# Block 0's experts chosen in two halves during the queries; scores of blocks 1 to 3 kept in SBUF for a later top-k

## Chip, cores, metric

One NeuronCore of a Trainium2 chip runs one launch. The metric is the device time of that launch in microseconds. Before the change three runs gave 1512.22, 1512.45 and 1513.83 us (median 1512.45).

## What is computed

A decoder layer for 512 tokens of width 1024, all in float32: RMS norm, one input projection, an mLSTM group and a latent-attention group, an output projection and a residual. The change touches only what follows, the PEER layer:

```python
qry = (xb @ w_q).reshape(TB, 8, 256)                 # 8 heads
s1 = einsum('thd,nd->thn', qry[..., :128], keys_1)   # 128 keys each
s2 = einsum('thd,nd->thn', qry[..., 128:], keys_2)
v1, i1 = top_k(s1, 16); v2, i2 = top_k(s2, 16)
cand = v1[..., :, None] + v2[..., None, :]           # 256 pairs
sc, ci = top_k(cand, 16)
idx = i1[ci // 16] * 128 + i2[ci % 16]               # 16384 experts
gate = softmax(sc)
act = gelu(einsum('thed,td->the', u_table[idx], xb))
y = einsum('the,thed->td', gate * act, v_table[idx])
```

## The kernel before, in words

The program is written out by hand for five engines, each with its own order, and kept in step by semaphores. The 512 tokens are four blocks of 128 (t = 0 to 3).

**Front** (0 to 290 us): projections, both attention groups, the output projection, and the normed h2 of each block. PSUM banks are handed round in the order of the list JOBS, eight at a time: a job's bank is free when the engine that takes it has read the job eight places earlier.

**Queries** (290 to 396 us). For each of 8 heads h: ScalarE rounds a part of w_q to float32r (wq_hi, round_q), GpSimd makes the rest (wq_lo, L709), TensorE makes two query tiles in three passes of 8 matmuls each (L1745, 24 matmuls a tile; the wait on wqlo_ready stands ahead of the first pass), and then the scores of all four blocks with 8 small matmuls (L1933). The scores stay in two PSUM banks ("s12", h, i), and VectorE takes from them, for each block and head, the 16 best of 128 keys twice (MAX8, FIND_INDEX8, MATCH_REPLACE8; L1440 to L1450). I call this one top-k.

**choose(t)** (L1456 to L1520, VectorE) makes out of the best keys of a block the 16 best experts of each head: sums (cand), a second top-k, and a search for the experts' numbers in which picked, 128x3200, is written and reduced twice, for 4 heads each time. choose(0) follows the last top-k and ends with idx0, for which GpSimd waits. choose(1) to choose(3) are cut into pieces that VectorE puts between other work, at PIECE_SIZE ns for each expert block.

**Dense products, pre** (blocks n = 0 to 71, 396 to about 670 us): tokens of blocks 1 to 3 (all but 32 tokens of block 1) are multiplied with all 16384 rows of u, 128 rows a block. For block n SyncE loads u_raw, ScalarE rounds it (u_hi, L981), GpSimd or VectorE makes u_lo (L718, L1526), TensorE runs 24 matmuls (L1952), the last 8 of which need u_lo, and ScalarE applies Gelu (L1019), for which TensorE waits two blocks later. GpSimd makes u_lo of the blocks below POOL_FIRST = 16, from SHARE_FROM = 20 on the even ones.

**Gathers and dots**: for block 0 (128 slots, "a") and for the 32 tokens left of block 1 ("b") the chosen rows of u are fetched: GpSimd issues an indirect DMA of 128 rows of 4 KB (gather_u, L734) into one of 8 buffers u_rows, VectorE multiplies and sums them with h2 (dot, L1543). A gather waits until the dot that used its buffer is done. The list DOTS says after which block which dots stand. The "a" dots read h2 of block 0 from two PSUM banks (h2_first, copied there by ScalarE, L1008), the "b" dots from SBUF (h2x).

**Main** (blocks 72 to 119, to 952 us) adds one-hot matmuls that spread the gates (L1598, L1991), **post** (blocks 120 to 127, to 986 us) prepares the second product, which fills TensorE to 1508 us: v_hi (L1095), v_lo (L1620), w (L1636, L1637), w_lo. DOTS puts two "a" dots after each of the blocks 120 to 123.

Of the kernel before, what the change touches and what calls it, by code (L numbers as in the profile page):

```python
# [92 lines left out]
POOL_FIRST, SHARE_FROM = 16, 20  # L93
# [9 lines left out]
DOTS = [""] * POST + ["aa"] * 4 + [""] * 4  # L103
# [7 lines left out]
assert "".join(DOTS).count("b") == NE  # L111
assert "".join(DOTS).count("a") == SLOTS
ORDER = [(kind, "".join(DOTS)[:x].count(kind)) for x, kind in enumerate("".join(DOTS))]
DOTS_PRE = len("".join(DOTS[:PRE]))
# [16 lines left out]
def front_jobs():  # L131
# [44 lines left out]
ENGINE_OF = dict(JOBS)  # L176

# [9 lines left out]
def build(nc, a):  # L187
    ctx = ExitStack()
    with ctx:
# [80 lines left out]
        wq_raw = [at(f"wq_raw{i}", kb, [P, KD, UNIT]) for i, kb in enumerate((42, 117.5, 106))]  # L270
        wq_hi = [at(f"wq_hi{i}", kb, [P, KD, UNIT], F32R) for i, kb in enumerate((126, 66))]
        wq_lo = [at(f"wq_lo{i}", kb, [P, KD, UNIT], F32R) for i, kb in enumerate((194, 74))]
        qryT = at("qryT", 186, [P, 3, S])
# [15 lines left out]
        pay_f = at("pay_f", 94, [P, 2, PH, TOPK])  # L289
# [195 lines left out]
        def _(sp):  # L485
# [31 lines left out]
            for h in range(PH):  # L517
                if h == 1:

                    sp.wait_ge(mixed_ready, 1)  # L520
# [3 lines left out]
                if h >= 3:  # L524

                    sp.wait_ge(wqlo_ready, h - 2)
# [14 lines left out]
            for j in range(1, 4):  # L541
                load_u(j, j)
# [126 lines left out]
        def _(pool):  # L669
# [36 lines left out]
            for h in range(PH):  # L706

                pool.wait_ge(wqhi_ready, h + 1)
                nc.gpsimd.tensor_tensor(wq_lo[h % 2][:], wq_raw[h % 3][:], wq_hi[h % 2][:].bitcast(F32),  # L709
                                        ALU.subtract).then_inc(wqlo_ready, 1)  # L710

            def split_u(n):

                pool.wait_ge(uhi_ready, n + 1)
                if n == 3:

                    arrived(pool, ("qry", PH - 1, 1))
# [3 lines left out]
            def gather_u(s):  # L721
# [3 lines left out]
                kind, x = ORDER[s]  # L725
                if kind == "b" and x == 0:
# [11 lines left out]
            for n in range(POOL_FIRST):  # L738
                split_u(n)
# [1358 lines left out]
```

## Time and profile before

| | |
|---|---|
| median of 3 runs | 1512.45 us |
| span of the profiled execution | 1512.2 us |
| runs beside it | 1512.22, 1512.45, 1513.83 us |
| TensorE busy | 97% (1473.2 us) |
| VectorE / ScalarE / GpSimd busy | 77% / 42% / 44% |
| mean granted clock of TensorE | 0.992 |
| chain that ended last | PE 73%, DVE 10%, DMA 9%, POOL 5% |

The profiled execution has no time of its own in the record beside its span; the fastest of the runs is 1512.22 us. In the profile PE is TensorE, DVE VectorE, ACT ScalarE, POOL GpSimd, SP SyncE. A timeline's row has start, duration, engine, line, operation, out<-in and shape; a bracket gives the idle time before it and what ended it.

### The profile page before, as it was taken

The page shows a single profiled execution, that of the slowest core. Times are in us where ns is not written, and L with a number is a line of the kernel's source. Part 1 is how long each engine was busy: PE and PEld are TensorE (multiplying, and loading weights), DVE is VectorE, ACT ScalarE, POOL GpSimd, SP SyncE. Part 2 cuts the span into 40 slices and gives each one's busy share as a digit, 9 for nine tenths or more (in the row PEclk, how much of TensorE's full clock was granted, in tenths as well). Part 3 has the DMA queues.
Part 4 walks back from the last instruction along what each step waited for, and adds up shares of the span by engine and source line. Part 5 has one row for each costly group of instructions (what it writes and reads, how often), then busy time and mean ns, then how long its engine had stood idle before and what let it go on. Part 6 is the DMA issues. An engine that isn't in the chain of part 4 may idle for free.

```text
span 1512.2 us, 23375 instructions
## 1 busy us (share of the span) xinstructions
PE 1473.2 (97%) x8069; PEld 1313.0 (87%) x8069; DVE 1161.3 (77%) x2378; ACT 640.6 (42%) x1058; POOL 665.2 (44%) x387
## 2 busy tenths in 40 slices
PE   6999989899999999999999999999999999999999
PEld 6879648788999999999999999988888888888887
DVE  4528473368999999879898889768878877877876
ACT  5363453222333333447777767434333224223221
POOL 3223150233586677865545545234443443443341
PEclk9999989999999999999999999999999999999999
DMA  6400202220569989999999999799999999999993
GB/s 205 147 29 1 112 1 70 88 74 25 173 207 354 328 313 341 415 356 360 354 361 362 349 365 397 293 333 382 383 354 352 347 352 347 354 347 349 351 345 123
DMA packets 182810, 408.19 MB, mean 270 GB/s; under 512 B 12725, under 2 KB 108725, under 8 KB 181209
## 3 DMA queue, kind: packets, MB, share of 16 engines
q1 hardware_dynamic: 141144, 256.36, 48.0%
q0 software_dynamic: 41600, 151.03, 26.3%
q8 instruction: 32, 0.52, 0.1%
q14 instruction: 34, 0.27, 0.0%
HBM read 359.03 MB, written 48.30 MB: 269 GB/s over the span
## 4 chain that ended last, share of the span: by engine, by line
PE 73%; DVE 10%; DMA 9%; POOL 5%; issue 2%; ACT 1%; SPq 0%; DVEq 0%; ACTq 0%; POOLq 0%
PE banks L1952 16%; PE banks L1745 16%; PE banks L2020 12%; PE banks L2021 12%; PE banks L2022 12%; DMA u_rows<-in_u,idx 7%; DVE gate_rows L1598 3%; POOL u_lo L718 3%; DVE u_rows L1543 2%; POOL u_rows L734 2%; DVE oh L1594 1%; DVE u_lo L1526 1%; PE banks L1933 1%; DMA u_raw<-in_uT 1%; PE banks L1796 1%
## 5 line engine op out<-in xcount | busy, mean ns | idle before, releaser
L766 POOL DMA_INDIRECT v_rows<-in_v,idx x128 | 203.5, 1590 | 324.4 <-DVE x_res L1682 274.6
L2020 PE MATMUL banks<-v_hi,w_hi 128*128 128x512 f32 x768 | 298.9, 389 | 0.0
L2021 PE MATMUL banks<-v_lo,w_hi 128*128 128x512 f32 x768 | 298.8, 389 | 0.0
L2022 PE MATMUL banks<-v_hi,w_lo 128*128 128x512 f32 x768 | 298.8, 389 | 0.0
L1095 ACT ACTIVATE v_hi<-v_raw 128x1024 fp32r<-128x1024 f32 x128 | 126.4, 1050 | 326.6 <-PE banks L2022 292.3
L734 POOL DMA_INDIRECT u_rows<-in_u,idx x160 | 190.4, 1190 | 139.7 <-DVE z L1543 106.3
L1620 DVE TENSOR_TENSOR v_lo<-v_raw,v_hi 128x1024 fp32r<-128x1024 f32 x128 | 153.5, 1221 | 95.2 <-ACT v_hi L1095 95.2
L718 POOL TENSOR_TENSOR u_lo<-u_raw,u_hi 128x1024 fp32r<-128x1024 f32 x66 | 163.9, 2486 | 90.4 <-ACT u_hi L981 49.7
L1952 PE MATMUL banks<-h_lo,u_hi 128*128 128x352 f32 x1024 | 197.5, 327 | 0.0
L1952 PE MATMUL banks<-h_hi,u_hi 128*128 128x352 f32 x1024 | 190.6, 328 | 0.0
L1952 PE MATMUL banks<-h_hi,u_lo 128*128 128x352 f32 x1024 | 187.0, 324 | 3.3 <-DVE u_lo L1526 3.3
L1543 DVE CUSTOM_DVE_ANT_0 u_rows<-u_rows,banks 128x1024 f32<-128x1024 f32 x128 | 152.2, 1220 | 28.7 <-DMA u_rows<-in_u,idx 28.7
L1952 PEld LDWEIGHTS banks<-h_hi,u_lo 128*128 128x128 f32 x1024 | 169.2, 188 | 3.6 <-DVE u_lo L1526 3.6
L2022 PEld LDWEIGHTS banks<-v_hi,w_lo 128*128 128x128 f32 x768 | 144.1, 188 | 30.2
L2020 PEld LDWEIGHTS banks<-v_hi,w_hi 128*128 128x128 f32 x768 | 144.1, 188 | 30.1 <-DVE v_lo L1620 0.3
L2021 PEld LDWEIGHTS banks<-v_lo,w_hi 128*128 128x128 f32 x768 | 144.1, 188 | 29.8
L1952 PEld LDWEIGHTS banks<-h_lo,u_hi 128*128 128x128 f32 x1024 | 167.0, 188 | 0.0
L1952 PEld LDWEIGHTS banks<-h_hi,u_hi 128*128 128x128 f32 x1024 | 166.6, 189 | 0.0
L1682 DVE SCALAR_TENSOR_TENSOR x_res<-v_rows,w,x_res 128x1024 f32<-128x1024 f32 x128 | 163.8, 1280 | 0.9
L981 ACT ACTIVATE u_hi<-u_raw 128x1024 fp32r<-128x1024 f32 x122 | 128.1, 1051 | 20.8 <-DMA u_raw<-in_uT 17.1
L1019 ACT ACTIVATE act_out<-banks 128x352 f32<-128x352 f32 x116 | 53.0, 457 | 143.8 <-PE banks L1952 133.8
L1991 PE MATMUL banks<-gate_rows,oh 128*128 128x128 f32 x768 | 101.3, 275 | 2.7 <-DVE gate_rows L1598 2.7
(269 smaller groups left out, 2072.6 us busy)
## 6 DMA issues: line engine op xcount, KB each, us to landing
u_raw<-in_uT SPq DMA_DIRECT2D x128, 512.0 KB
v_raw<-in_v SPq DMA_DIRECT2D x128, 512.0 KB
gate_scratch<-stage SPq DMA_DIRECT2D x12, 2048.0 KB
gates<-gate_scratch SPq DMA_DIRECT2D x29, 768.0 KB
act_scratch<-act_out SPq DMA_DIRECT2D x116, 176.0 KB
act_in<-act_scratch SPq DMA_DIRECT2D x29, 704.0 KB, 6.7
wi_raw<-in_w_in SPq DMA_DIRECT2D x8, 1024.0 KB, 8.8
wq_raw<-in_w_q SPq DMA_DIRECT2D x8, 1024.0 KB, 5.5
```

The source lines that it names most:

```text
L718: nc.gpsimd.tensor_tensor(u_lo[:, n % 4, :, :], u_raw[:, n % 4, :, :], u_hi[:, n % 4, :, :].bitcast(F32), ALU.subtract).then_inc(ulo_pool, 1)
L734: nc.gpsimd.indirect_dma_start(u_rows[U_SLOT[s]][:], None, a["u"], bass.IndirectOffsetOnAxis(ap=at_x, axis=0)).then_inc(ug_in[U_SLOT[s]], 16)
L766: nc.gpsimd.indirect_dma_start(v_rows[s % V_ROWS][:], None, v_flat, bass.IndirectOffsetOnAxis(ap=idx0[:, s:s + 1], axis=0)).then_inc(vg_in ...
L981: nc.scalar.activation(u_hi[:, j % 4, :, :], u_raw[:, j % 4, :, :], ACT.Copy).then_inc(uhi_ready, 1)
L1543: nc.vector.tensor_tensor_reduce(rows[:], rows[:], h2, 1.0, 0.0, ALU.mult, ALU.add, z[:, x:x + 1]).then_inc(dot_done, 1)
L1620: nc.vector.tensor_tensor(v_lo[q][j][:], v_raw[:, j, :], v_hi[q][:, j, :].bitcast(F32), ALU.subtract).then_inc(vlo_ready, 1)
L1682: nc.vector.scalar_tensor_tensor(out=x_res[:, 0, :], in0=v_rows[n % V_ROWS][:], scalar=w0[:, n:n + 1], in1=x_res[:, 0, :], op0=ALU.mult, o ...
L1745: last = mm(o, lhs(x, k), rhs(y, k), start=n == k == 0, stop=n == 2 and k == KD - 1)
L1952: last = mm(o, u[:, q, k, :], h2[:, k, T1:], start=m == 0, stop=m == PER_BLOCK - 1)
L2020: mm(y, w, v_hi[q][:, j, ds], start=first and j == 0, stop=False)
L2021: mm(y, w, v_lo[q][j][:, ds], start=False, stop=False)
L2022: end = mm(y, w_lo[q][:, j, t * P:(t + 1) * P], v_hi[q][:, j, ds], start=False, stop=last and j == GROUP - 1)
```

## The change

Scores of block 0 get a bank of their own ("s0", h), which VectorE reads as before and frees halfway through its top-k; those of block 1 ("s13", h, 0) and of blocks 2 and 3 ("s13", h, 1) are copied by ScalarE to scores_1 and scores_23 in SBUF. In the queries VectorE does the top-k of block 0 and of block 1 only. After head 3 it runs choose on heads 0 to 3 of block 0; then, after each of the heads 4 to 7, six dots, 24 in all, which read h2 of block 0 from SBUF (h2_nat). The other half of choose(0), the last top-k of block 1, the top-k of blocks 2 and 3 and choose(1) to choose(3) become pieces of the pre stage; FREE_SIZE = 85000 ns of them come before block 30. GpSimd makes u_lo of all blocks below 32. 24 "a" dots leave their later places: 16 of the pre stage and the 8 of post; 3 "b" dots move from pre to main. wq_lo is written over wq_raw, buffers move, and h2x is loaded only when 24 dots are done.

```diff
-POOL_FIRST, SHARE_FROM = 16, 20
+POOL_FIRST, SHARE_FROM = 32, 32
+EARLY = 24
+EARLY_STEP = 6
...
-DOTS = [""] * POST + ["aa"] * 4 + [""] * 4
+DOTS = [""] * E_BLOCKS
...
-for _n in [*range(PRE - 25, PRE, 2), *range(PRE + 1, PRE + 32, 2), PRE + 4, PRE + 14, PRE + 24]:
+for _n in [*range(PRE - 19, PRE, 2), *range(PRE + 1, PRE + 32, 2), *range(PRE + 4, PRE + 28, 4)]:
     DOTS[_n] += "b"
-for _n in [*range(PRE - 14, PRE, 4), *range(PRE + 32, POST)]:
+for _n in range(PRE + 32, POST):
     DOTS[_n] += "a"
+FREE_SIZE = 85000
...
-        jobs += [(("s12", h, i), "D") for i in range(2)]
+        jobs += [(("s0", h), "D")] + [(("s13", h, i), "A") for i in range(2)]
...
@@ SyncE
-            sp.wait_ge(wqlo_ready, PH)
+            arrived(sp, ("qry", PH - 2, 1))
             load_u(0, 0)
-            arrived(sp, ("qry", PH - 2, 1))
...
                     sp.wait_ge(h2x_saved, 16)
+                    sp.wait_ge(dot_done, EARLY)
...
@@ GpSimd
-            for n in range(POOL_FIRST):
-                split_u(n)
-            pool.wait_ge(idx_ready, 1)
-            s = 0
+            for h in range(PH - 1):
+                split_query(h)
+            pool.wait_ge(idx_ready, 1)
+            for s in range(U_ROWS):
+                gather_u(s)
+            split_query(PH - 1)
+            for s in range(U_ROWS, U_ROWS + 2 * EARLY_STEP):
+                gather_u(s)
+            split_u(0)
+            split_u(1)
+            for s in range(U_ROWS + 2 * EARLY_STEP, U_ROWS + 3 * EARLY_STEP):
+                gather_u(s)
+            split_u(2)
+            for s in range(U_ROWS + 3 * EARLY_STEP, U_ROWS + EARLY):
+                gather_u(s)
+            for n in range(3, POOL_FIRST):
+                split_u(n)
...
@@ VectorE
+                if n < EARLY:
+                    h2 = h2_nat[:, 0, :]
...
-            for _ in choose(0):
-                pass
+            for h in range(PH // 2):
+                top_k(0, h)
+                if h:
+                    top_k(1, h - 1)
+            for _ in choose(0, 0, PH // 2):
+                pass
+            top_k(1, PH // 2 - 1)
+            for h in range(PH // 2, PH):
+                top_k(0, h)
+                if h > PH // 2:
+                    top_k(1, h - 1)
+                for _ in range(EARLY_STEP):
+                    dot()
```

**GpSimd, from the split of the last query to the splits of the products.** Before: all query splits, 16 product splits (u_lo), then the wait for idx and the gathers (idx is idx0, in_u the table u).

```order
L709 TENSOR_TENSOR wq_lo_112<-wq_raw_107,wq_hi_110 128x2048 [waits wqhi_ready]
L718 TENSOR_TENSOR u_lo<-u_raw,u_hi 128x1024 [waits uhi_ready] x3
L718 TENSOR_TENSOR u_lo<-u_raw,u_hi 128x1024 [waits bank_done,uhi_ready]
L718 TENSOR_TENSOR u_lo<-u_raw,u_hi 128x1024 [waits uhi_ready] x12
L734 DMA u_rows_150<-in_u,idx_146 128x1024 [waits idx_ready]
L734 DMA u_rows_151<-in_u,idx_146 128x1024
```

After the change, the same place ("..." stands for the gathers of the buffers between):

```order
L729 TENSOR_TENSOR wq_lo_109<-wq_raw_106,wq_hi_113 128x2048 [waits wqhi_ready]
L754 DMA u_rows_154<-in_u,idx_150 128x1024 [waits idx_ready]
...
L754 DMA u_rows_161<-in_u,idx_150 128x1024
L729 TENSOR_TENSOR wq_lo_110<-wq_raw_107,wq_hi_114 128x2048 [waits wqhi_ready]
L754 DMA u_rows_154<-in_u,idx_150 128x1024 [waits dot_done]
...
L754 DMA u_rows_157<-in_u,idx_150 128x1024 [waits dot_done]
L735 TENSOR_TENSOR u_lo<-u_raw,u_hi 128x1024 [waits uhi_ready] x2
...
L754 DMA u_rows_155<-in_u,idx_150 128x1024 [waits dot_done]
L735 TENSOR_TENSOR u_lo<-u_raw,u_hi 128x1024 [waits uhi_ready]
...
L754 DMA u_rows_161<-in_u,idx_150 128x1024 [waits dot_done]
L735 TENSOR_TENSOR u_lo<-u_raw,u_hi 128x1024 [waits uhi_ready] x29
```

The first 32 gathers now stand ahead of the product splits: 8 ahead of the split of query 7, 12 more ahead of u_lo of blocks 0 and 1, 6 ahead of block 2, 6 ahead of block 3 (the first of the 29). From the ninth on each gather waits for a dot.

**VectorE, from the numbers of the experts on.** Before, choose(0) ends with the cast to idx after all 32 head and block pairs have had their top-k, and choose(1) and a product split follow:

```order
L1494 TENSOR_TENSOR picked<-pay,sc_f 128x3200 [waits dve_step]
L1498 TENSOR_REDUCE e_f<-picked 128x64 [waits dve_step]
L1503 CAST idx_146<-e_f 128x128 [waits dve_step]
L1456 TENSOR_SCALAR pay_f<-best_i 128x128
L1457 CAST pay_f<-best_i 128x128
```

After the change, the end of the first half of choose(0), the start of a top-k of block 1 from SBUF, of one of block 0 from PSUM, and the six dots (ISA with h_nat; h_nat is the name at the address of h2_nat):

```order
L1548 TENSOR_TENSOR picked<-pay,sc_f 128x3200
L1552 TENSOR_REDUCE e_f<-picked 128x64 [waits dve_step]
L1557 CAST idx_150<-e_f 128x64 [waits dve_step]
L1491 MAX best_v<-scores_116 128x8 [waits bank_freed_scalar]
...
L1491 MAX best_v<-banks 128x8 [waits bank_done,dve_step]
...
L1599 ISA u_rows_154,z_151<-u_rows_154,h_nat 128x1024 [waits ug_in0,dve_step]
...
L1599 ISA u_rows_159,z_151<-u_rows_159,h_nat 128x1024 [waits ug_in5]
L1599 ISA z_151 128x1
L1491 MAX best_v<-banks 128x8 [waits bank_done]
```

After each six dots come two top-k, the first of which waits for TensorE's scores of the next head; the last six dots follow the top-k of head 7.

## Rows read from the trace of the kernel before

**Rows 1.** The chain of waits, query and pre stage: start, us, what, matmuls

```profile
309.79 1.78 PE banks L1933 x16
...
374.97 10.90 PE banks L1745 x48
...
395.85 205.22 PE banks L1952 x1296
```

**Rows 2.** Two stretches: busy us of PE, PEld, DVE, ACT, POOL; clock, DMA share, GB/s

```profile
340.00:360.00 20.00, 20.00 (x98) 16.87 (x97) 17.93 (x105) 5.40 (x5) 7.01 (x2) 1.00 0.07 26
640.00:660.00 20.00, 20.00 (x127) 19.98 (x127) 14.56 (x25) 7.17 (x10) 12.03 (x8) 1.00 0.96 380
```

**Rows 3.** VectorE's timeline: two top-k and choose(0)

```profile
310.72 0.50 DVE L1440 MAX8 best_v<-banks 128x8 f32<-128x128 f32 x2 [19.10 <-PE banks L1933]
...
313.62 0.50 DVE L1440 MAX8 best_v<-banks 128x8 f32<-128x128 f32 x2
...
410.48 0.78 DVE L1456 TENSOR_SCALAR pay_f<-best_i 128x128 f32<-128x128 uint32 x1
411.89 3.18 DVE L1465 TENSOR_TENSOR cand<-best_v 128x128 f32<-128x128 f32 x7
...
423.19 3.48 DVE L1494 TENSOR_TENSOR picked<-pay,sc_f 128x3200 f32<-128x3200 f32 x1
426.71 3.48 DVE L1498 TENSOR_REDUCE e_f<-picked 128x64 f32<-128x3200 f32 x1
...
497.88 0.99 DVE L1465 TENSOR_TENSOR cand<-best_v 128x128 f32<-128x128 f32 x7
```

**Rows 4.** GpSimd's timeline: a query split, and a gather (its issue)

```profile
357.58 4.57 POOL L709 TENSOR_TENSOR wq_lo<-wq_raw,wq_hi 128x2048 fp32r<-128x2048 f32 x1 [8.09 <-ACT wq_hi L782]
...
450.33 0.93 POOL L734 DMA_INDIRECT u_rows<-in_u,idx  x1 [0.30 <-issue]
```

**Rows 5.** Timelines of VectorE and GpSimd where h2x dots meet GpSimd

```profile
601.01 1.21 DVE L1543 CUSTOM_DVE_ANT_0 u_rows<-u_rows,h2x 128x1024 f32<-128x1024 f32 x1
...
600.16 1.74 POOL L734 DMA_INDIRECT u_rows<-in_u,idx  x1 [0.31 <-issue]
...
695.34 1.22 DVE L1543 CUSTOM_DVE_ANT_0 u_rows<-u_rows,banks 128x1024 f32<-128x1024 f32 x1
...
696.48 1.40 DVE L1543 CUSTOM_DVE_ANT_0 u_rows<-u_rows,h2x 128x1024 f32<-128x1024 f32 x1
...
694.39 2.42 POOL L718 TENSOR_TENSOR u_lo<-u_raw,u_hi 128x1024 fp32r<-128x1024 f32 x1 [1.35 <-DVE opened L1563]
```

**Rows 6.** A DMA's landing: tile h2x; and u_rows in the chain of waits

```profile
DMA to landing us min/median/max: 3.0/3.1/4.2
...
766.89 10.20 DMA u_rows<-in_u,idx
```

**Rows 7.** ScalarE's timeline: copy of h2, then the first Gelu

```profile
398.58 1.03 ACT L1008 ACTIVATE banks<-h_nat 128x1024 f32<-128x1024 f32 x1 [2.95 <-DVEq L1452]
...
401.90 0.47 ACT L1019 ACTIVATE act_out<-banks 128x352 f32<-128x352 f32 x1
```

**Rows 8.** TensorE's timeline after two long waits

```profile
290.39 3.78 PE L1745 MATMUL banks<-h_hi,wq_hi 128*128 128x512 f32 x8 [0.69 <-ACT h_hi L938]
...
298.75 1.98 PE L1745 MATMUL banks<-h_hi,wq_hi 128*128 128x512 f32 x8
...
975.28 2.50 PE L1952 MATMUL banks<-h_hi,u_lo 128*128 128x352 f32 x8 [3.28 <-DVE u_lo L1526]
...
979.50 1.43 PE L1952 MATMUL banks<-h_lo,u_hi 128*128 128x352 f32 x8
```

**Rows 9.** Timelines of ScalarE and VectorE ahead of TensorE's wait at 972 us

```profile
967.01 2.00 ACT L1095 ACTIVATE v_hi<-v_raw 128x1024 fp32r<-128x1024 f32 x2
...
970.06 2.35 DVE L1620 TENSOR_TENSOR v_lo<-v_raw,v_hi 128x1024 fp32r<-128x1024 f32 x2
...
974.00 1.22 DVE L1526 TENSOR_TENSOR u_lo<-u_raw,u_hi 128x1024 fp32r<-128x1024 f32 x1
```

More of the change, by code:

```diff
@@ L517, in _ @@
             for h in range(PH):
-                if h == 1:
+                if h == 0:
                     sp.wait_ge(mixed_ready, 1)
@@ L725, in gather_u @@
                 kind, x = ORDER[s]
+                if kind == "a" and x == SLOTS // 2:
+                    pool.wait_ge(idx_ready, 2)
                 if kind == "b" and x == 0:
@@ L1454, in choose, with top_k @@
-            def choose(t):
-                step(nc.vector.tensor_scalar(pay_f[:, 0, :, :], best_i[:, 0, t, :, :], float(NK), None, ALU.mult))
-                step(nc.vector.tensor_copy(pay_f[:, 1, :, :], best_i[:, 1, t, :, :]))
+            def top_k(t, h):
+                j = ("s13", h, 0 if t == 1 else 1) if t else ("s0", h)
+                if t:
+                    emptied(dve, j)
+                else:
+                    arrived(dve, j)
+                from_at = scores[t][:, h, :] if t else bank(j)
+                sc = [from_at[:, s * NK:(s + 1) * NK] for s in range(2)]
+                bv = [best_v[:, s, t, h, :] for s in range(2)]
+                bi = [best_i[:, s, t, h, :] for s in range(2)]
+                for s in range(2):
+                    step(nc.vector.max(bv[s][:, 0:8], sc[s]))
+                settle()
+                for s in range(2):
+                    step(nc.vector.max_index(bi[s][:, 0:8], bv[s][:, 0:8], sc[s]))
+                    step(nc.vector.match_replace(best_tmp[:, s, :], bv[s][:, 0:8], sc[s], LOWEST))
+                settle()
+                if not t:
+                    dve.sem_inc(freed["D"], 1)
+                for s in range(2):
+                    step(nc.vector.max(bv[s][:, 8:16], best_tmp[:, s, :]))
+                settle()
+                for s in range(2):
+                    step(nc.vector.max_index(bi[s][:, 8:16], bv[s][:, 8:16], best_tmp[:, s, :]))
+                settle()
@@ L1567, in splits_and_dots, with routing @@
                     dot()
[L1569 to L1574 removed]
+            def routing():
+                pieces = choose(0, PH // 2, PH)
+                for size in HALF_SIZES:
+                    next(pieces)
+                    yield size
+                assert next(pieces, 0) == 0
+                top_k(1, PH - 1)
+                yield TOPK_SIZE
+                for t in range(1, TB):
+                    if t > 1:
+                        for h in range(PH):
+                            top_k(t, h)
+                            yield TOPK_SIZE
+                    pieces = choose(t)
+                    for size in CHOOSE_SIZES:
+                        next(pieces)
+                        yield size
+                    assert next(pieces, 0) == 0
+            work, done = routing(), 0
+            for n in range(POOL_FIRST - 2, PRE):
+                while done < FREE_SIZE + (n - POOL_FIRST + 3) * PIECE_SIZE:
+                    size = next(work, None)
+                    if size is None:
+                        break
+                    done += size
                 splits_and_dots(n)
```

170 lines of the change are left out of this document (86 added, 84 removed).

## Prediction

> **What bounds the kernel now.** I read the page first: TensorE is busy for 97% of the span, VectorE for 77%, the others for less than half, and TensorE's amount of work (matmuls, columns, order) is not touched by the change. So the change can gain only where TensorE waits, and loses whatever new wait it gives TensorE. Second the chain of waits: from 309.79 us on, a head of the query stage is two tiles (10.90 us) and its scores (1.78 us), 12.68 us, one after the other without a gap, and from 395.85 us the first 54 blocks (1296 matmuls) take 205.22 us, 3.80 us a block [rows 1]. Third the windows: in the queries TensorE is busy 20.00 of 20 us while VectorE has 17.93, and at 640 us VectorE is down to 14.56 [rows 2]. VectorE's top-k, the work that the change moves, thus lies beside TensorE's work already, and moving it gains nothing by itself. The one wait ahead of the second product is in post: 3.28 us for u_lo of block 125, and after it TensorE runs slowly for 4 us [rows 8]. What can go wrong lies in the queries: the change puts work on two queues, GpSimd's and VectorE's, on whose results TensorE waits at once.
>
> **Step 1: when the first half of choose(0) ends.** Scores of block 0, head 3, are there at 309.79 + 3 x 12.68 + 0.55 (their quarter of 1.78 us and 0.1) = 348.4 [rows 1]. Two top-k of 2.90 us each [rows 3] bring VectorE to 354.2. The small steps of choose(0) took 423.19 - 410.48 = 12.7 us for 8 heads, of them 2.2 because cand took 3.18 us there and 0.99 at 497.88, and some 0.5 at pay_f; half of the 10.0 left and a little for fixed cost is 5.4. picked and its reduction are 3.48 us each and stay whole for 4 heads [rows 3]. Without a collision that is 354.2 + 5.4 + 7.0 + 0.2 = 366.8. But picked reads two tiles in SBUF and comes at 359.6, inside GpSimd's split of query 6 (357.58 to 362.15 [rows 4]); I let it wait (see step 3): 369.3.
>
> **Step 2: GpSimd.** From 369.4 it issues 8 gathers at 0.93 + 0.30 us [rows 4], the last few against dots, to 381.6, and only then the split of query 7, 4.57 us [rows 4]: 386.2. TensorE has that tile due at 374.97 + 5.45 = 380.4 [rows 1]: the first new wait, 5.9 us (1.0 without collisions).
>
> **Step 3: the loop of gathers and dots.** Gather s waits for dot s-8, and 32 gathers stand ahead of the split of block 3; so this split waits for dot 23, the last early one. Between 369.3 and dot 23 VectorE has eight top-k, 8 x 2.90 = 23.2 us, and 24 dots at 1.14 us (695.34 to 696.48 [rows 5]), 27.4 us: 419.9 with no wait at all. Now the collisions. An "a" dot read h2 from PSUM; the early ones read both operands from SBUF, like the dots with h2x. The gather that met one took 1.74 us in place of 0.93 and ended 0.89 us after that dot's start, and a dot with h2x that met a product split took 1.40 in place of 1.21 [rows 5]. So I walk the two queues forward with three rules: a dot, picked and a GpSimd split exclude each other; a gather's end waits for the first 0.87 us of a dot; data land 3.3 us after the issue, a little over the 3.1 us of h2x [rows 6]. The walk: dots 0 to 5 end at 381.9, 6 to 11 at 395.8, 12 to 17 (behind the splits of blocks 0 and 1) at 412.8, 18 to 23 at 426.0; u_lo of blocks 0, 1, 2, 3 is ready at 406.0, 409.3, 419.2 and **431.2**. TensorE needed the last at 395.85 + 3 x 3.80 + 2.53 (16 of 24 matmuls) = 409.8. The delay is 431.3 - 409.8 = **21.5 us**. On TensorE it shows as 5.9 (query 7), 1.9 (block 0), 7.0 (block 2) and 6.8 (block 3). The 7.0 is ScalarE's: its copy of h2 needs the bank of head 7's scores of block 0, which VectorE frees at 414.4, and from copy to first Gelu pass 3.8 us [rows 7].
>
> **Bounds of step 3.** Without any collision the same walk gives 12.0 us (dot 23 at 417.3, u_lo of block 3 at 421.6). With each dot holding off a gather for its whole 1.14 us it gives 27.5. With landings of 8 us (in main they reach 10.20 [rows 6]) it gives 25.9. I take 21.5, because the two rows that show collisions are of the same instruction pair as here. The floor is firm: head 7's scores come at 399.1, then stand two top-k, six dots, a gather and a split, 5.8 + 6.8 + 1.2 + 2.4 us, which with 0.1 makes 415.4 and a delay of 5.6 us even if nothing else ever waited.
>
> The Trainium skill (SBUF — State Buffer, section "SBUF: two separate sides") says that VectorE and GpSimd share a port pair as an exclusive lock: an instruction of VectorE with two SBUF inputs and a GpSimd one block each other, for the whole instruction of whichever starts first. By that rule the sum would carry 27.5 us in place of 21.5; the gather above went on 0.3 us before its dot ended, so the trace agrees with the lock and only in part with its length.
>
> **Step 4: the clock.** After waits of this kind TensorE ran slowly: the first query tile took 298.75 - 290.39 = 8.4 us in place of 5.4, and after 972 us 16 matmuls took 4.22 us (975.28 to 979.50) in place of 2.53 [rows 8]. After the last new wait I add the middle of 3.0 and 1.7, **2.4 us**; after the waits before it the slow stretch lies inside the next wait and costs nothing.
>
> **Step 5: post.** The dots of blocks 120 to 123 go. The last two stand ahead of v_lo at 970.06 and so of u_lo at 974.00, for which TensorE waited. ScalarE has the rounded v for it at 968.0 [rows 9], so v_lo can start at 968.1 and 1.9 of the 3.28 us go: **-1.9**. What is left, 1.4 us, is far shorter than the waits behind which a slow stretch is on record, so I count step 4's 1.7 us as gone too: **-1.7**. At worst the gate rows from HBM, which VectorE needs next, come late and both stay: 0.
>
> **At nothing.** The top-k of blocks 2 and 3 (16 x 2.90 = 46 us), the other half of choose(0) and one top-k more come to VectorE in pre; 10 product splits, 16 "a" and 3 "b" dots and the first half leave it. From 426 us on it has until block 72 half of choose(0) 12.6, 17 top-k 49.3, three choose of some 26, 21 splits 25.6, 52 dots 59.3 and the norms 5: 230 us, and block 72 starts near 693: 37 us spare. The cover before was the idle share at 640 us [rows 2]; if it fails, u_lo of odd blocks comes late, a few us. GpSimd's 16 more splits of 2.4 us fit under 3.8 us a block. ScalarE's 16 score copies go beside queries. SyncE's new wait for the 24 dots (426) has the load of block 8 behind it, which waits for u_lo of block 4 (434) anyway and is due on TensorE at 448: no cost. Three "b" dots more in main: within VectorE's gaps.
>
> **Sum** against the profiled span: 1512.2 + 21.5 + 2.4 - 1.9 - 1.7 = **1532.5 us**; the span lies 0.25 us below the median of the runs.
>
> **Rivals.** (a) As above, 1532.5: 0.46. (b) The collisions cost next to nothing, so that 12.0 stands for 21.5: 1523.0. For it: the pairs of rows that show them are few, and other instructions may have stretched them; against it: the two pairs of rows in [rows 5]. 0.22. (c) The lock at full length: 27.5 us, 1538.5; for it, picked and splits stretch each other too; 0.22. (d) The early part reaches TensorE only at the floor, 5.6 us, no slow stretch: 1512.2 + 5.6 - 3.6 = 1514.2; it needs VectorE never late, against the sum of 419.9: 0.04. (e) Faster: gathers and dots keep ahead of TensorE, and only post changes: 1508.6. The point at which this decides is u_lo of block 3 at 409.8 us; dot 23 would have to end by 406.0, 13.9 us sooner than VectorE's own work allows: 0.04. (f) The change doesn't do what it says, its gathers landing so late that the dots wait for data (8 us): 25.9 us, 1536.9: 0.02.
>
> **Numbers.** A difference under 0.2% (3.0 us) can't be told from no change here. Faster is (e), 0.04; within is (d), 0.04; slower the rest, 0.92. The range leaves out (d) and (e), and goes from 1519, which is (b) without the clock's 2.4 us and 1.6 us off its choose, to 1541, (c) with the upper end of the clock (0.6) and half of step 5 (1.8).
>
> **What would show it.** In the profile after: the split of query 7 ends at 386 and TensorE waits for it at 380; a wait for Gelu or for the h2 copy ahead of block 2; u_lo of block 3 ready near 431 and TensorE's wait there named POOL u_lo; a granted clock of 0.5 behind it; gathers of 1.3 to 1.8 us among the early dots; the wait at 972 (then near 995) of 1.4 us. The forecast is wrong if the first 54 blocks start within 3 us of 395.85 and go at 3.80 each.

## The result, and the profile after

The changed kernel takes 1538.38 us (median of 4 runs, 1537.48 to 1540.2) against 1512.34 us before (4 runs, 1510.18 to 1513.83): ratio 1.0179, 95% interval 1.016 to 1.0199. It is slower by 1.8%. The profiled execution after has a span of 1536.6 us, 24.4 more than before, at a mean granted clock of 0.984.

TensorE's waits, from the view of the waits (total, times, longest us):

```profile
...
PE banks L2040 <- ACT act_out L1067: 9.5, 1, 9.5
PE banks L2040 <- POOL u_lo L735: 7.2, 2, 6.2
...
PE banks L1834 <- POOL wq_lo L729: 5.2, 1, 5.2
...
PE banks L2040 <- DVE u_lo L1580: 1.0, 1, 1.0
```

Four new ones stand in the first three rows shown, 21.9 us together. The last row is what is left of the wait for u_lo of block 125 [rows 8]. TensorE's timeline shows where they lie: the first tile of query 7, the third pass of block 0, the first of block 2, the third of block 3, and post.

```profile
384.54 3.78 PE L1834 MATMUL banks<-h_hi,wq_hi 128*128 128x512 f32 x8 [5.16 <-POOL wq_lo L729]
...
392.84 1.95 PE L2021 MATMUL banks<-keysT,qryT 128*128 128x128 f32 x16
...
406.56 1.54 PE L2040 MATMUL banks<-h_hi,u_lo 128*128 128x352 f32 x8 [1.04 <-POOL u_lo L735]
...
421.42 2.68 PE L2040 MATMUL banks<-h_hi,u_hi 128*128 128x352 f32 x8 [9.52 <-ACT act_out L1067]
...
435.84 2.72 PE L2040 MATMUL banks<-h_hi,u_lo 128*128 128x352 f32 x8 [6.17 <-POOL u_lo L735]
...
443.67 1.43 PE L2040 MATMUL banks<-h_hi,u_hi 128*128 128x352 f32 x8
...
1001.44 1.54 PE L2040 MATMUL banks<-h_hi,u_lo 128*128 128x352 f32 x8 [1.05 <-DVE u_lo L1580]
```

Before, the third pass of block 3 started at 409.62 us (TensorE's timeline: 395.60 is the start of block 0). So 26.2 us are lost by then, although the first scores came 1.05 us sooner (308.58 against 309.63). From 435.84 to 443.67 four passes took 7.83 us; at 1.267 each (3.80 us a block, [rows 1]) they would take 5.07, so the slow clock behind the last wait cost 2.8 us. The windows show it and its two forerunners; the columns are as in [rows 2], the third number from the right is the granted clock:

```profile
384.00:388.00 4.00, 3.46 (x8) 2.78 (x9) 4.00 (x7) 0.00 (x0) 3.54 (x3) 0.50 0.66 227
...
420.00:424.00 4.00, 2.58 (x9) 2.61 (x10) 3.90 (x14) 3.51 (x5) 2.48 (x2) 0.50 0.94 341
436.00:440.00 4.00, 4.00 (x14) 4.00 (x15) 4.00 (x1) 0.46 (x1) 4.00 (x2) 0.50 0.94 268
```

0.50 is the lower of the two clocks, 1.2 GHz, and each time TensorE had just stood still. In post the wait is 2.2 us shorter than in [rows 8], and no slow stretch follows (the pass takes 1.54 us where it took 2.50), which gives 1.7 us. 26.2 + 2.8 - 2.2 - 1.7 = 25.1 us, against 24.4 measured. The 0.7 us between them can be placed. From block 6 to block 110 the change is 28.98 us behind at each block's start, so nothing in pre or in most of main adds to the delay. Then two waits for gate rows, 2.7 us before, are gone, but TensorE's passes behind them are slower in the change (1.33 us in place of 1.27, see the last section), which takes back some 2 us. Ahead of the wait in post the change is 28.3 us behind (998.90 against 970.57), and 28.3 - 2.2 - 1.7 = 24.4.

The two queues behind this, GpSimd's and VectorE's timelines. GpSimd's rows are three gathers, the split of query 7 and two gathers among dots. VectorE's first row is a small copy in choose(0), the others are the fourth of the early dots, which met that split, then the fifth, the sixth and the seventh:

```profile
368.93 1.12 POOL L754 DMA_INDIRECT u_rows<-in_u,idx  x1 [7.83 <-DVE idx L1557]
...
372.85 0.94 POOL L754 DMA_INDIRECT u_rows<-in_u,idx  x1 [0.30 <-issue]
...
378.02 1.94 POOL L754 DMA_INDIRECT u_rows<-in_u,idx  x1 [0.30 <-issue]
379.99 4.50 POOL L729 TENSOR_TENSOR wq_lo<-wq_raw,wq_hi 128x2048 fp32r<-128x2048 f32 x1
384.65 1.75 POOL L754 DMA_INDIRECT u_rows<-in_u,idx  x1 [0.16 <-issue]
386.71 1.98 POOL L754 DMA_INDIRECT u_rows<-in_u,idx  x1 [0.30 <-issue]
```

```profile
358.97 2.17 DVE L1540 COPY tops<-sc_v 128x4 f32<-128x4 f32 x1
...
379.33 6.25 DVE L1599 CUSTOM_DVE_ANT_0 u_rows<-u_rows,h_nat 128x1024 f32<-128x1024 f32 x1 [0.18 <-DMA u_rows<-in_u,idx]
...
385.51 1.21 DVE L1599 CUSTOM_DVE_ANT_0 u_rows<-u_rows,h_nat 128x1024 f32<-128x1024 f32 x1
...
386.66 1.22 DVE L1599 CUSTOM_DVE_ANT_0 u_rows<-u_rows,h_nat 128x1024 f32<-128x1024 f32 x1
...
393.68 1.22 DVE L1599 CUSTOM_DVE_ANT_0 u_rows<-u_rows,h_nat 128x1024 f32<-128x1024 f32 x1
```

The dot at 379.33 ends at 385.58, 1.1 us after the split, though its row begins 0.66 us before the split's: the start of a row does not tell which of two goes first. The gather at 386.71 began 0.05 us after a dot and ended at 388.69, 0.8 us after that dot's end. From 379.3 to the end of dot 23 at 428.5 VectorE has no wait of note.

### The profile page after: what moved, and what is told of

Same layout as the page of the kernel before. It is cut to its first block, busy times and chain, and to the rows that moved or that the text cites. A ratio compares the mean times of both kernels' runs of the same rounds, so it can differ in the third digit from the quotient of the medians.

```text
span 1536.6 us, 23312 instructions
## 1 busy us (share of the span) xinstructions
PE 1481.7 (96%) x8069; PEld 1320.3 (86%) x8069; DVE 1176.1 (77%) x2383; ACT 648.4 (42%) x1074; POOL 691.3 (45%) x397
## 4 chain that ended last, share of the span: by engine, by line
PE 89%; DVE 7%; ACT 1%; POOL 1%; issue 1%; DMA 1%; DVEq 0%; ACTq 0%
PE banks L2040 31%; PE banks L1834 13%; PE banks L2109 11%; PE banks L2107 11%; PE banks L2108 11%; PE banks L2078 6%; DVE u_rows L1599 2%; POOL u_rows L754 1%; PE banks L1885 1%; DVE wo_lo L1402 1%; PE banks L1944 1%; PE banks L1963 0%; PE banks L1969 0%; PE banks L1891 0%; DMA u_rows<-in_u,idx 0%
## 5 line engine op out<-in xcount | busy, mean ns | idle before, releaser
L735 POOL TENSOR_TENSOR u_lo<-u_raw,u_hi 128x1024 fp32r<-128x1024 f32 x76 | 191.4, 2524 | 91.4 <-DVE opened L1631 64.3
L1014 ACT ACTIVATE u_hi<-u_raw 128x1024 fp32r<-128x1024 f32 x122 | 128.1, 1051 | 15.5 <-DMA u_raw<-in_uT 14.6
L1599 DVE CUSTOM_DVE_ANT_0 u_rows<-u_rows,banks 128x1024 f32<-128x1024 f32 x104 | 122.8, 1214 | 4.8 <-DMA u_rows<-in_u,idx 4.6
L1687 DVE TENSOR_SCALAR gate_rows<-consts,tab 128x128 f32<-128x128 f32 x384 | 105.2, 356 | 11.1 <-PE banks L2078 6.9
```

What stands on the lines that cost most here:

```text
L735: nc.gpsimd.tensor_tensor(u_lo[:, n % 4, :, :], u_raw[:, n % 4, :, :], u_hi[:, n % 4, :, :].bitcast(F32), ALU.subtract).then_inc(ulo_pool, 1)
L1014: nc.scalar.activation(u_hi[:, j % 4, :, :], u_raw[:, j % 4, :, :], ACT.Copy).then_inc(uhi_ready, 1)
L1599: nc.vector.tensor_tensor_reduce(rows[:], rows[:], h2, 1.0, 0.0, ALU.mult, ALU.add, z[:, x:x + 1]).then_inc(dot_done, 1)
```

## The experiments

They ran on three chips, on which even the kernel before spread over 1506 to 1518 us, and the changed kernel, on one of them, over 1534 to 1549. So the totals are read with their intervals, and the early part is read from each trace: the start of block 3's third pass, 409.62 us before and 435.84 in the change.

**The change again.** Unchanged.

> The changed kernel as it is, beside the others on this chip. The runs here spread over 10 us in place of 3, and in some profiles a u block took 4.00 us in place of 3.80 at an unchanged granted clock. If that is of the chip and the moment, the change lies at 1535 to 1545 us here with block 3's third pass at 435 to 439 us; if block 3's third pass lies elsewhere, the trace of the change that the other runs are read against was not typical.

Measured: 1544.76 us (1534.48 to 1549.06), ratio 1.023 (1.0198 to 1.0262).

```profile
406.12 1.54 PE L2040 MATMUL banks<-h_hi,u_lo 128*128 128x352 f32 x8 [2.13 <-POOL u_lo L735]
...
421.00 2.69 PE L2040 MATMUL banks<-h_hi,u_hi 128*128 128x352 f32 x8 [9.54 <-ACT act_out L1067]
...
435.41 2.72 PE L2040 MATMUL banks<-h_hi,u_lo 128*128 128x352 f32 x8 [5.88 <-POOL u_lo L735]
```

The same waits to within 1.1 us, and block 3 at 435.4. The early part repeats; the total is what varies here.

**Query 7 first.** Is the wait for wq_lo a loss of its own?

```diff
-            for h in range(PH - 1):
+            for h in range(PH):
                 split_query(h)
             pool.wait_ge(idx_ready, 1)
             for s in range(U_ROWS):
                 gather_u(s)
-            split_query(PH - 1)
```

> The changed kernel, but GpSimd splits the weights of query 7 ahead of the first eight gathers. Theory A, the chain of dots decides: VectorE had no idle time between the first gathers and dot 23, so the end of dot 23 and with it u_lo of block 3 hardly move; TensorE's 5.2 us for wq_lo go, and the waits behind them (Gelu 9.5, u_lo 6.2) grow by about as much. What can be won is the slow clock behind the wait for wq_lo and the 5.0 us by which that split stretched a dot, less the 4.6 us by which the gathers now start later: 1534 to 1539 us. Rival B, TensorE's waits simply add up, each with its own cause: the 5.2 us go and so do some 2.7 us of slow clock behind them: 1530.5 us. If A holds, the wait for wq_lo is gone from the trace and the wait for Gelu is 12 to 15 us.

Measured: 1548.37 us (1541.48 to 1556.53), ratio 1.0225 (1.0163 to 1.0286).

```profile
392.45 3.75 PE L1833 MATMUL banks<-h_hi,wq_hi 128*128 128x512 f32 x8 [5.49 <-issue]
...
425.12 2.68 PE L2039 MATMUL banks<-h_hi,u_hi 128*128 128x352 f32 x8 [7.39 <-ACT act_out L1066]
...
439.37 2.71 PE L2039 MATMUL banks<-h_hi,u_lo 128*128 128x352 f32 x8 [6.13 <-POOL u_lo L735]
```

The wait for wq_lo is gone, and TensorE waits 5.5 us at the second tile of query 7 instead. The profile names no releaser. In the code that tile needs the bank of head 5's scores of block 0, which VectorE frees in a top-k behind the first six dots. Block 3 comes 3.5 us later, as the first gather is issued at 374.3 in place of 368.9. Theory A holds in substance (nothing is won), though not for the wait for Gelu, which was to grow and fell to 7.4 us; B is out. The total lies above A's 1539 as well: in the profiled execution TensorE was 32.8 us behind the kernel before at block 5 and 44.6 at block 64, as each block took 4.00 us in place of 3.80 (last section).

**Top-k before dots.** The same question for the wait for Gelu.

```diff
                 top_k(0, h)
+                if h == PH - 1:
+                    for _ in range(EARLY_STEP):
+                        dot()
                 if h > PH // 2:
                     top_k(1, h - 1)
-                for _ in range(EARLY_STEP):
-                    dot()
+                if h != PH - 2:
+                    for _ in range(EARLY_STEP):
+                        dot()
```

> The changed kernel, but VectorE does the six dots behind head 6 only after the top-k of block 0, head 7, so that the bank of these scores is free sooner for ScalarE's copy of h2. Theory A, the waits of TensorE are stations of one chain: the wait for Gelu falls from 9.5 to 3 us or less, and the waits for u_lo of blocks 2 and 3 grow by 4 to 9 us; block 3's third pass starts within 3 us of the 435.8 us that it had. Rival B, the wait for Gelu is a cause of its own: block 3's third pass starts at 428 us or sooner.

Measured: 1538.63 us (2 runs), ratio 1.0179 (1.0148 to 1.0211).

```profile
406.05 2.48 PE L2044 MATMUL banks<-h_hi,u_lo 128*128 128x352 f32 x8 [3.48 <-POOL u_lo L735]
...
422.56 2.71 PE L2044 MATMUL banks<-h_hi,u_lo 128*128 128x352 f32 x8 [6.79 <-POOL u_lo L735]
...
434.38 2.72 PE L2044 MATMUL banks<-h_hi,u_lo 128*128 128x352 f32 x8 [5.79 <-POOL u_lo L735]
```

The 9.5 us for Gelu are gone, the waits for u_lo have grown from 7.2 to 16.0 us in all, and block 3 moved by 1.5 us. The waits are stations of one chain.

**Dots with one input.** What do the collisions cost? These 24 dots leave out the multiplication with h2.

```diff
+                if n < EARLY:
+                    nc.vector.tensor_reduce(z[:, x:x + 1], rows[:], AX_X, ALU.add).then_inc(dot_done, 1)
+                    return
```

> The changed kernel, but the 24 early dots only sum the gathered row, with one input in SBUF; the multiplication with h2 is left out of these 24. Number, place and order of gathers, dots and splits stay. Theory A, collisions of two-input instructions with GpSimd make up about half of the delay (two dots were stretched by 5.0 and 2.2 us, and nine gathers of 24 took 1.7 to 2.0 us in place of 0.94): dots are near 1.1 us each, the gathers 0.94, u_lo of block 3 comes some 9 to 13 us sooner, and the whole takes 1523 to 1529 us. Rival B, the order of the two queues does it and collisions are part of the picture only: 1535 us or more. Rival C, a reduction with one input holds GpSimd off as well: gathers of 1.7 us and more remain, and the time is within 2 us of 1538.

Measured: 1535.09 us (1528.22 to 1540.41), ratio 1.0145 (1.0094 to 1.0195). From the groups of instructions between 368 and 434 us (busy us, mean ns), first the change, then this kernel:

```profile
L754 POOL DMA_INDIRECT u_rows<-in_u,idx x32 | 40.0, 1251 | 20.6 <-issue 8.4 <-DVE idx L1557 7.8 <-DVE z L1599 4.4
L1599 DVE CUSTOM_DVE_ANT_0 u_rows<-u_rows,h_nat 128x1024 f32<-128x1024 f32 x24 | 35.4, 1526 | 1.3 <-issue 1.0 <-DMA u_rows<-in_u,idx 0.2
```

```profile
L754 POOL DMA_INDIRECT u_rows<-in_u,idx x32 | 30.2, 944 | 17.8 <-issue 8.7 <-DVE idx L1557 7.8 <-DVE z L1600 1.1
L1600 DVE TENSOR_REDUCE z<-u_rows 128x1 f32<-128x1024 f32 x24 | 27.8, 1212 | 2.1 <-DMA u_rows<-in_u,idx 1.8 <-issue 0.2
```

The gathers take 0.94 us in the mean: GpSimd spends 9.8 us less on them and VectorE 7.6 less on its dots. That excludes C. But block 3 comes at 429.71, only 6.1 us sooner, and not 9 to 13 as in A. Part of the rest went into something new, in TensorE's timeline in the middle of the last query tile:

```profile
399.42 0.40 PE L1837 MATMUL banks<-h_hi,wq_lo 128*128 128x512 f32 x1 [2.32 <-issue]
400.14 0.40 PE L1837 MATMUL banks<-h_hi,wq_lo 128*128 128x512 f32 x1 [0.33 <-issue]
```

TensorE stops there for 3.0 us in all with no releaser, and the pass goes on slowly; another stop of this kind, 2.3 us, stands ahead of block 2. What they are stays open. In sum the collisions are worth about 6 us here, more if these stops are a chance event; 20 us of the delay stay without them, which is B's side: the order of the two queues does most of it. The total of 1535 us is above theory A's 1529 and at B's lower end; the single runs reach from 1528 to 1540.

**Half of the early dots.** Three behind each head in place of six.

```diff
-EARLY = 24
-EARLY_STEP = 6
+EARLY = 12
+EARLY_STEP = 3
...
+for _n in range(31, 67, 3):
+    DOTS[_n] += "a"
...
-FREE_SIZE = 85000
+FREE_SIZE = 100000
```

> The changed kernel with 12 early dots in place of 24, three behind each head in place of six; the other 12 go to pre, one every third block from 31 on, and VectorE's free time ahead of block 30 is counted as 100 us in place of 85. Theory A, the chain through both queues decides: GpSimd has 20 gathers ahead of the split of block 3 in place of 32 and VectorE 12 dots less (14 to 18 us), so that VectorE has idle time and u_lo of block 3 is ready near 414 to 419 us; the wait for wq_lo stays, as the first eight gathers still stand ahead of it. 1516 to 1524 us. Rival B, the loss is one of place (any gather in the queries) and not of number: 1530 us or more.

Measured: 1546.06 us (1544.05 to 1551.33), ratio 1.0224 (1.0198 to 1.025). Block 3's third pass starts 15.9 us sooner than in the change, and that of block 2 waits 1.8 us:

```profile
413.97 1.54 PE L2042 MATMUL banks<-h_hi,u_lo 128*128 128x352 f32 x8 [1.83 <-POOL u_lo L737]
...
419.99 1.55 PE L2042 MATMUL banks<-h_hi,u_lo 128*128 128x352 f32 x8 [0.35 <-POOL u_lo L737]
```

For the early part A is right: each of the 12 dots and gathers less is worth 1.3 us, where A had about 1. The total is far off, and TensorE's timeline tells where most of it went. TensorE is 10.5 us behind the kernel before up to block 32 and 27.7 us at block 36, as there is a wait in block 32:

```profile
545.49 2.71 PE L2042 MATMUL banks<-h_hi,u_lo 128*128 128x352 f32 x8 [15.03 <-POOL u_lo L737]
```

GpSimd had waited 23.9 us for "opened", the mark by which VectorE lets it make u_lo of block 32. I read that as my 100 us of routing ahead of block 30 and tried again with 95:

```diff
-FREE_SIZE = 100000
+FREE_SIZE = 95000
...
-PIECE_SIZE = 1800
+PIECE_SIZE = 1500
```

> The run with half of the early dots again (12 in the queries, three behind each head, 12 in pre), without what spoiled it: there VectorE did 100 us of routing ahead of block 30 and opened GpSimd's split of block 32 fifteen us late. Now 95 us, and 1.5 us of routing per block behind it in place of 1.8. Theory A, the early loss goes with the number of gathers ahead of the split of block 3, about 1 us for each: block 3's third pass near 424 us again, against 435.8 in the change and 409.6 before, no long wait at block 32, and 1522 to 1528 us. Rival B, pre has no room for 12 dots beside the moved top-k: block 3 as in theory A, and behind it waits for u_lo or gate rows that sum to 5 us or more, 1530 us and above.

Measured: 1539.7 us (1535.4 to 1546.02), ratio 1.0196 (1.0163 to 1.0229). Block 3's third pass starts at 420.68, after a wait of 4.11 us. The 424 us that the theories gave for it fit block 4's third pass of the run before (423.90); block 3's was at 419.99. At block 32 there are still 9.1 us:

```profile
541.88 2.71 PE L2042 MATMUL banks<-h_hi,u_lo 128*128 128x352 f32 x8 [9.13 <-POOL u_lo L737]
```

In the change itself, block 32 is close as well: GpSimd's timeline has

```profile
542.53 2.42 POOL L735 TENSOR_TENSOR u_lo<-u_raw,u_hi 128x1024 fp32r<-128x1024 f32 x1 [6.97 <-DVE opened L1631]
```

so u_lo of block 32 is ready at 544.95, and TensorE takes it at 548.80 (435.84 + 29 x 3.80 and the 2.8 us of slow clock). Only 3.9 us are spare, and that while TensorE is 29 us late. With half of the early dots most of the gain is lost again at block 32: TensorE is 12.8 us behind ahead of it and 25.4 at block 36, and then 31.0 at block 64, as its blocks take 4.00 us (last section). So theory B holds for the total, by that wait. That a smaller FREE_SIZE would mend it was not tried.

**No early dots, twice.** First all 24 behind the queries.

```diff
-                for _ in range(EARLY_STEP):
-                    dot()
...
+            for n in range(POOL_FIRST):
+                split_u(n)
+                if 4 <= n < 4 + EARLY:
+                    gather_u(U_ROWS + n - 4)
...
+            for _ in range(EARLY):
+                at = done
+                while done < at + TOPK_SIZE:
+                    done += next(work)
+                dot()
```

> The changed kernel with its 24 early dots behind the query stage: all query and the first four u splits on GpSimd come ahead of the further gathers, then one gather per block, and VectorE does one such dot per top-k in pre, reading h2 from PSUM. The scores in SBUF, the choice of block 0 in halves and the empty post stay. Theory A, the early gathers and dots are the whole loss: the waits for wq_lo, Gelu and u_lo of blocks 0 to 3 are gone, post's gain stays (2.2 and 1.8 us by the trace of the change) and the front's 1.0 us: 1507 to 1510 us. Rival B, the scores through ScalarE and the top-k in pre cost something of their own: then 1513 us or more, with TensorE waiting for u_lo of an odd block between 32 and 72, or for tri.

Measured: 1536.63 us (1531.51 to 1542.44), ratio 1.0146 (1.0106 to 1.0186). Block 3's third pass starts at 409.72, as before. So the early gathers and dots are the whole of the early loss. But then TensorE waits nine times for u_lo, 17.1 us in all, and GpSimd's timeline says why:

```profile
436.70 0.95 POOL L753 DMA_INDIRECT u_rows<-in_u,idx  x1 [4.19 <-DVE z L1588]
437.68 2.35 POOL L734 TENSOR_TENSOR u_lo<-u_raw,u_hi 128x1024 fp32r<-128x1024 f32 x1
```

A gather waits for the dot that frees its buffer, and the next split stands behind it. The second version has a gather behind every second split only, and 12 of the dots in later blocks (not in GpSimd's way until block 31).

```diff
+                if n >= 6 and n % 2 == 0 and n < 6 + 2 * EARLY:
+                    gather_u(U_ROWS + n // 2 - 3)
...
+                while done < at + 2 * TOPK_SIZE:
```

> The changed kernel with no dot in the queries: the weights of query 7 first, then eight gathers, and 12 further gathers of block 0, one behind every second u split from block 6 on; VectorE does those 12 dots after every second top-k in pre, 12 more stand in pre, one every third block from 31 on. It mends what the run with all 24 behind the queries did: there GpSimd had a gather behind each split and TensorE waited nine times for u_lo, 17.1 us. Theory A, GpSimd's load was all that was wrong there: no wait for u_lo of more than 1 us up to block 31, and the post stage as in the change: 1507 to 1512 us. Rival B, the 46 us of top-k that now lie in pre do not fit: waits for u_lo of odd blocks or for tri between blocks 32 and 72, 1516 us or more.

Measured: 1540.95 us (1539.01 to 1545.64), ratio 1.0205 (1.0178 to 1.0232). Block 3 at 408.71, and then again waits, the longest 3.57 us ahead of 477.49 and 5.80 us ahead of 621.75, each for u_lo of GpSimd:

```profile
474.12 0.95 POOL L755 DMA_INDIRECT u_rows<-in_u,idx  x1 [7.51 <-DVE z L1590]
475.08 4.70 POOL L736 TENSOR_TENSOR u_lo<-u_raw,u_hi 128x1024 fp32r<-128x1024 f32 x2
```

A is out, and B holds in a wider form: VectorE does not get the moved top-k and the dots done in time, and as GpSimd's gathers wait for the dots, the u splits pay. From 410 to 530 us VectorE is busy for 118.18 and 117.90 of 120 us in these two runs, and for 117.23 in the change; the idle time comes behind that. So the 37 us that I had counted as spare are not there when they are needed. In the change, where nothing in pre waits for VectorE, it is busy for 257.80 of the 270 us from 430 to 700, where the forecast had 230 of 267.

**One wait alone, before.** ScalarE's copy of h2 eleven times, in the kernel before.

```diff
+            for k in range(11):
+                if k:
+                    act.wait_ge(h2_placed, k)
                 nc.scalar.activation(h2_first, h2_nat[:, 0, :], ACT.Copy).then_inc(h2_placed, 1)
...
```

> The kernel before, but ScalarE copies h2 to PSUM eleven times, one after the other, in place of once, so that the first Gelu and TensorE's block 2 come late. This makes one wait of TensorE, for Gelu, of 9.5 to 11 us (ten copies of 1.0 to 1.1 us, less the 1.1 us that it was early), and nothing else. Theory A, a slow stretch behind a wait is paid each time: the time is 1512.3 plus the wait plus 2 to 3 us, 1524.5 to 1526, and the granted clock is 0.5 for some 4 us behind the wait. Rival B, the stretch costs nothing where TensorE has its other work in hand and only the last wait counts: 1512.3 plus the wait, 1522 to 1523.

Measured: 1523.85 us (1518.3 to 1536.28), ratio 1.0095 (1.0061 to 1.0129).

```profile
411.83 2.69 PE L1955 MATMUL banks<-h_hi,u_hi 128*128 128x352 f32 x8 [9.64 <-ACT act_out L1022]
414.32 2.37 PE L1955 MATMUL banks<-h_lo,u_hi 128*128 128x352 f32 x8
416.53 1.43 PE L1955 MATMUL banks<-h_hi,u_lo 128*128 128x352 f32 x8
```

The two passes behind the wait take 4.70 us in place of 2.53. A wait of 9.6 us that stands alone costs 9.6 + 2.2 in this trace, as A has it. The median is 11.1 us above before, between the two theories, with an interval that holds both; so A rests on the trace.

**Post alone.** The kernel before, with its eight post dots moved to pre.

```diff
-DOTS = [""] * POST + ["aa"] * 4 + [""] * 4
+DOTS = [""] * E_BLOCKS
...
-for _n in [*range(PRE - 14, PRE, 4), *range(PRE + 32, POST)]:
+for _n in [*range(PRE - 30, PRE, 4), *range(PRE - 15, PRE, 4), *range(PRE + 32, POST)]:
```

> The kernel before with one thing of the change alone: the eight dots of blocks 120 to 123 go, into pre (four more and another pattern of the four that were there). Theory A, what the trace of the change showed for post comes alone as well: the wait for u_lo of block 125 falls from 3.3 to about 1.0 us and the slow stretch behind it (16 matmuls in 4.2 us) goes: 3 to 4.3 us faster than before, ratio 0.997 to 0.998. Rival B, post gained in the change because something else was early there (the gate rows, VectorE's lighter main): within 1 us of before, and the wait for u_lo stays near 3 us. Rival C, the eight dots have no room in pre: new waits there, slower.

Measured: 1515.75 us (12 runs, 1512.33 to 1518.38), ratio 1.0029 (1.0014 to 1.0045). In post the wait is 1.33 us and no slow pass follows, as A has it; and in pre and main stand

```profile
677.68 2.08 PE L1991 MATMUL banks<-gate_rows,oh 128*128 128x128 f32 x8 [4.62 <-DVE gate_rows L1598]
```

and three more of the kind, 7.6 us in all, where the kernel before has two, 2.7 us. C: by the medians the dots cost more where they went than they had cost in post (3.3 us slower). The profiled execution, 1512.6 us, is one of the fastest of the twelve, so it shows where time goes and not how much in the median.

**Splits earlier, before.** The dots stay; u_lo of block 125 is made ahead of the last two, those of blocks 126 and 127 move ahead as well, and ScalarE rounds w a block later.

```diff
             split_u(POST + 4)
+            split_u(POST + 5)
             post_dots(POST + 3)
             for k in range(2, 4):
                 split_v(0, 0, k)
+            split_u(POST + 6)
             dve.wait_ge(dot_done, len(ORDER))
             weights(0, 0)
-            split_u(POST + 5)
+            split_u(POST + 7)
             split_w(0, 0)
-            split_u(POST + 6)
-            split_u(POST + 7)
... ScalarE
-                if j == 4:
+                if j == 5:
                     round_w(0, 0)
```

> The kernel before with its dots where they were; in post VectorE makes u_lo of block 125 right behind that of block 124, ahead of two dots, two v_lo and the weights, u_lo of block 126 ahead of the weights, that of block 127 ahead of w_lo, and ScalarE rounds w one block later. Theory A, in post TensorE waits only because this split stands last in VectorE's queue (its u_hi is there at 966.8, and it is needed at 972.0): the 3.3 us go and the 1.7 us of slow clock behind them, less what w_lo may come late (0 to 2 us): 1507 to 1510 us, ratio 0.996 to 0.9985, faster than both. Rival B, the wait moves to w_lo of the first group, 3 us or more ahead of the second product: within 2 us of before.

Measured: 1503.98 us (12 runs, 1499.16 to 1511.96), ratio 0.9958 (0.9939 to 0.9977). No wait is left in post, nor ahead of the second product (VectorE's timeline: the two splits in one row, then w_lo, done at 977.98, 2.0 us before the second product starts at 979.95):

```profile
964.95 2.35 DVE L1526 TENSOR_TENSOR u_lo<-u_raw,u_hi 128x1024 fp32r<-128x1024 f32 x2
...
976.22 1.76 DVE L1644 TENSOR_TENSOR w_lo<-w,w_hi 128x1536 fp32r<-128x1536 f32 x1 [0.42 <-ACT w_hi L1099]
```

This version is faster than both kernels, and theory A holds: post gives 3.3 + 1.7 = 5.0 us, the interval of the runs 3 to 9. The median lies somewhat below A's 1507.

## Why the prediction was right, and where it was not

It forecast slower, 1532.5 us in a range of 1519 to 1541; measured are 1538.4. By its steps:

**Step 1** gave 369.3 for the first half of choose(0); with the front 1.05 us sooner, 368.3. The first gather starts at 368.93. It was the copy of tops that GpSimd's split of query 6 held off (2.17 us, to 361.14; the split ran from 356.54 to 361.11), not picked, with the same effect.

**Step 2** gave 5.9 us for the split of query 7; measured 5.2.

**Step 3** had the four waits in their places with their releasers: 5.9, 1.9, 7.0 and 6.8 against 5.2, 1.0, 9.5 and 6.2, in sum 21.6 against 21.9. The delay of block 3, though, was 21.5 in the forecast and is 26.2 (27.3 without the front's 1.05). This term was mis-sized, in two places. The first is the landing of the gathered rows, which I set at 3.3 us from h2x [rows 6]. The row of the fourth dot was issued at 372.85 and was there at 379.3, 6.5 us later. So VectorE was still at its first dots when GpSimd came to the split of query 7, where my walk had dots 0 to 5 done at 381.9 and no collision; a dot was held 5.0 us, and dot 5 ended at 387.8. The second is the tail: I let GpSimd follow dot 23 closely, 5.2 us from its end to u_lo of block 3. It is 7.3 us (428.5 to 435.8), because more of the gathers still stood in the queue, held off before (three were begun behind dot 23).

No run changed the landing alone, so how the excess divides between the two is argued. The 6.5 us lie nearer to the 8 us of rival (f), which I gave 0.02, than to my 3.3. Nor is the floor of 5.6 us firm: it holds the 5.9 us for wq_lo, and without them nothing is left of it.

On the collisions themselves I had read [rows 5] wrongly. By the times, the gather at 600.16 was not held by the dot behind it but by the instruction ahead, in VectorE's timeline before:

```profile
599.88 1.21 DVE L1526 TENSOR_TENSOR u_lo<-u_raw,u_hi 128x1024 fp32r<-128x1024 f32 x1
```

It is a split with two inputs in SBUF that ran to 601.0; the gather ended at 601.9, 0.8 us after it, beside the dot. The gathers of the change show the same: held to the end of the dot that runs, then done beside the next (the one at 384.65 ends at 386.40, and the dot at 385.51 takes its usual 1.21 us). The Trainium skill (SBUF — State Buffer, section "SBUF: two separate sides") says that the lock is held for the whole instruction. The trace agrees for a dot that meets a split (6.25 us) and for a gather that meets a dot, but not for the dot that follows: the end of a held gather does not hold it. Rival (c), 1538.5 us, was built on that length and lies within 0.2 us of the median; its 27.5 us stand against 27.3. But the run with one-input dots shows that the lock accounts for about 6 us of it, where the forecast had 21.5 - 12.0 = 9.5 us and (c) 15.5. So the queues' own work is larger than my walk had it, some 21 us in place of 12.0, and (c) came near by a sum of two errors. My 1532.5 is helped by the same luck: a lock counted too high stands against a walk that was too short.

**Step 4** gave 2.4 us behind the last wait; measured 2.8. That the earlier slow stretches cost nothing holds, with a reason now shown: query 7's tile took 8.3 us in place of 5.4, yet VectorE did not wait for TensorE after 379 us, and both runs that took one of TensorE's waits away left block 3 within 3.5 us. A wait that stands alone does pay for its slow stretch, 2.2 us.

**Step 5** gave -1.9 and -1.7; measured -2.2 and -1.7. Both runs on the kernel before confirm the cause, VectorE's queue ahead of u_lo of block 125.

**At nothing**: what stood there did cost nothing in the change (28.98 us behind at block 6 and at block 110), but the 37 us spare up to block 72 were the wrong measure. The first deadline is block 32, with 3.9 us to spare while TensorE is 29 us late. Had the early part gone well, as in rivals (d) and (e), time would probably have been lost there; the runs with fewer early dots point to it, but each of them also changed VectorE's order in pre.

## What to carry to other kernels

Where an in-order queue makes what the critical engine waits for, each instruction put ahead of it that waits for another engine ties the two together: removing one of the waits then only shows the next. Before dots or gathers are moved to fill an engine, look in post or wherever a wait stands at the order of that engine's queue: three splits moved ahead by a few places, and one rounding moved back, gave 6 us (3 to 9 by the interval), and moving the dots away cost more than it gave. And measure spare time to the next deadline, not to the end of the stage.

## What the runs showed of the hardware that I had not expected

A gather that GpSimd issues while VectorE runs an instruction with two SBUF inputs is mostly held up to that instruction's end, and ends 0.8 to 0.9 us after it even when the next such instruction follows at once. Two gathers of the change that began 0.03 and 0.04 us after a dot were not held, and there the dot took 1.29 us in place of 1.22; the first of them and its dot:

```profile
397.15 0.94 POOL L754 DMA_INDIRECT u_rows<-in_u,idx  x1 [0.30 <-issue]
```

```profile
397.12 1.29 DVE L1599 CUSTOM_DVE_ANT_0 u_rows<-u_rows,h_nat 128x1024 f32<-128x1024 f32 x1
```

A reduction with one input does not hold a gather: 0.94 us in the mean of 32. But a copy with one input, that of tops, 128x4, was held by a split for 2.17 us.

At a granted clock of 1.00 and with TensorE busy throughout, the same matmuls came at different rates in different executions, and this carries much of the spread of the totals. The windows from 500 to 600 us of the change again, and of the run with query 7 first:

```profile
500.00:600.00 100.00, 100.00 (x633) 100.00 (x632) 97.72 (x376) 37.91 (x53) 63.86 (x35) 1.00 0.74 264
```

```profile
500.00:600.00 100.00, 100.00 (x602) 100.00 (x601) 88.86 (x334) 35.55 (x51) 62.09 (x32) 1.00 0.72 241
```

633 against 602 matmuls in 100 us are 3.80 and 4.00 us a block, or 1.27 and 1.33 us a pass of 8. The rate changes inside an execution as well, where TensorE has waited or matmuls of another kind come between. In the change a pass takes 1.27 us from 442 us on and 1.33 from 678 on, where nine matmuls of another kind come in (in the kernel before from 649 on, at the same block), and the wait of 1.05 us in post ends the slower stretch. The passes at 997.57 and 998.90 lie 1.33 us apart, those at 1002.82 and 1004.08, behind the wait, 1.26. In both runs with half of the early dots the slower rate begins behind the long wait at block 32. I found no engine or transfer in the profile that accounts for it, and what sets the rate is open.
